# Linear attention's masked level blocks: one strided sum replaced by half masks, an add and four accumulated matmuls

## The reference, cut to what matters

```
G      = cumsum(log_a)                                # per frame and key channel
scores = sum_d q[n,d] * k[m,d] * exp(-|G[n,d] - G[m,d]|)
o      = scores @ v + (q * exp(G)) @ state
state  = exp(G_last) * state + (k * exp(G_last - G))^T @ v
```

## Time and profile before

| what | value |
|---|---|
| median of 3 runs | 2629.23 us |
| profiled execution: span from first to last instruction | 2625.6 us (the page gives no time of it beside the span) |
| mean granted TensorE clock | 0.972 |
| busy, TensorE matmul / weight load | 2446.7 (93%) / 1964.3 us (75%) |
| busy, VectorE | 808.3 us (31%) |
| busy, ScalarE | 402.1 us (15%) |
| busy, GpSimd | 1317.4 us (50%) |

### The profile page before, as it was taken

One profiled execution on the slowest core, in us unless ns is written; L12 is line 12 of the kernel. 1 busy time (PEld: TensorE's weight loads), 2 busy tenths in 40 slices (PEclk: granted clock), 3 DMA queues, 4 the chain that ended last, 5 costly groups with the idle time before them and its releaser, 6 DMA issues. The chain is left out here.

```text
span 2625.6 us, 28086 instructions
## 1 busy us (share of the span) xinstructions
PE 2446.7 (93%) x10712; PEld 1964.3 (75%) x10712; DVE 808.3 (31%) x917; ACT 402.1 (15%) x581; POOL 1317.4 (50%) x711
## 2 busy tenths in 40 slices
PE   6999999999999998766898998898899999999988
PEld 5888788888888887666774664676788888888776
DVE  3000240000000004999327336226532222232333
ACT  3000110010001002222002002002321111111201
POOL 3434343333333333555559598577253333347774
PEclk9999999999999999888999999999999999999999
DMA  4323222222222250121444434444222222234333
GB/s 155 100 92 105 79 95 98 96 96 96 96 96 96 96 209 32 57 71 42 144 161 144 146 126 144 160 140 156 96 83 73 74 74 72 74 133 140 141 121 144
DMA packets 137741, 285.77 MB, mean 109 GB/s; under 512 B 10689, under 2 KB 60097, under 8 KB 137682
## 3 DMA queue, kind: packets, MB, share of 16 engines
q1 hardware_dynamic: 137106, 282.90, 31.0%
q10 hardware_dynamic: 576, 2.10, 0.2%
HBM read 207.36 MB, written 77.59 MB: 109 GB/s over the span
## 5 line engine op out<-in xcount | busy, mean ns | idle before, releaser
L353 POOL TENSOR_TENSOR w_hi<-w_raw,zero_col 128x1024 fp32r<-128x1024 f32 x233 | 448.7, 1926 | 1080.3 <-PE psum L319 1064.6
L317 PE MATMUL psum<-act_hi,w_hi 128*128 128x512 f32 x2128 | 834.0, 392 | 15.5 <-DVE act_lo L386 6.1
L318 PE MATMUL psum<-act_lo,w_hi 128*128 128x512 f32 x2128 | 832.6, 391 | 0.0
L319 PE MATMUL psum<-act_hi,w_lo 128*128 128x512 f32 x2128 | 832.2, 391 | 0.0
L356 POOL TENSOR_TENSOR w_lo<-w_raw,w_hi 128x1024 fp32r<-128x1024 f32 x233 | 576.0, 2472 | 18.3
L317 PEld LDWEIGHTS psum<-act_hi,w_hi 128*128 128x128 f32 x2128 | 402.6, 189 | 102.0 <-issue 14.5
L319 PEld LDWEIGHTS psum<-act_hi,w_lo 128*128 128x128 f32 x2128 | 402.3, 189 | 84.2
L318 PEld LDWEIGHTS psum<-act_lo,w_hi 128*128 128x128 f32 x2128 | 402.6, 189 | 83.7
L863 DVE TENSOR_TENSOR q_lev<-e_t,g_x 128x896 f32<-128x896 f32 x32 | 52.4, 1639 | 660.6 <-ACT e_t L741 660.5
L317 PE MATMUL psum<-w_hi,d_hib 128*128 128x512 f32 x480 | 193.3, 403 | 23.5 <-DVE d_lob L1526 20.6
L318 PE MATMUL psum<-w_lo,d_hib 128*128 128x512 f32 x480 | 192.1, 400 | 0.0
(11 more groups left out here) (137 smaller groups left out, 2162.9 us busy)
## 6 DMA issues: line engine op xcount, KB each, us to landing
w_raw<-in_w_stream SPq DMA_DIRECT2D x233, 512.0 KB, 3.3
proj_scratch<-stage SPq DMA_DIRECT2D x64, 512.0 KB, 2.6
r_x<-proj_scratch SPq DMA_DIRECT2D x64, 256.0 KB, 3.0
value_scratch<-stage SPq DMA_DIRECT2D x24, 512.0 KB, 4.6
ffn_scratch<-u_fb SPq DMA_DIRECT2D x22, 512.0 KB, 2.7
d_raw<-ffn_scratch SPq DMA_DIRECT2D x44, 256.0 KB, 3.6
r_v<-value_scratch SPq DMA_DIRECT2D x32, 256.0 KB, 3.3
x_tok<-in_x SPq DMA_DIRECT2D x4, 1024.0 KB, 8.0
```

The lines of the kernel that those rows point to most:

```text
L317: nc.tensor.matmul(o, s_hi, m_hi, start=start, stop=False)
L318: nc.tensor.matmul(o, s_hi, m_lo, start=False, stop=False)
L319: return nc.tensor.matmul(o, s_lo, m_hi, start=False, stop=stop)
L353: nc.gpsimd.tensor_tensor(w_hi[:, j, :], w_raw[:, j, :], zero_col[:, :].to_broadcast((P, D)), ALU.add).then_inc(sem["hi_split"], 1)
```

## The change

The mask is cut into two instructions of 512 columns. The first writes four masked blocks into `s_sum[:, h, :]`, the second the other four into `s_half`; an add on VectorE puts the second onto the first. The strided sum over the blocks is gone: `outputs` multiplies each of the four remaining blocks with the same values and lets PSUM accumulate them. `s_sum` (512 columns for each of four heads) and `s_half` (512) take the place of `s_masked` (1024) and `p_t` (128 for each head). The waits move: that for the outputs of the tile before stands ahead of the first mask, that for the head before ahead of the second, and TensorE's next scores wait for the second mask. The `begin_phase` of the first head comes ahead of its mask.

```diff
-g_S g_mask g_P g_kT g_kd ...
+g_S g_mask0 g_mask1 g_P g_kT g_kd ...
...
-            s_masked = sb(s, "s_masked", (P, (NL + 1) * P))
+            s_sum = sb(s, "s_sum", (P, HEADS, HALF))
+            s_half = sb(s, "s_half", (P, HALF))
             g_kdt = sb(s, "g_kdt", (P, GLA_QK))
-            p_t = sb(s, "p_t", (P, HEADS, P))
...
                 def scores(h):
                     e = 4 * t + h
                     dve.wait_ge(sem["g_S"], e + 1)
-                    if not (first and h == 0):
-                        dve.wait_ge(sem["g_P"], e)
-                    nc.vector.tensor_tensor(s_masked[:, :], bank[:, 3 * HALF:5 * HALF], masks[:, :],
-                                            ALU.mult).then_inc(sem["g_mask"], 1)
-                    dve.wait_ge(sem["g_mask"], e + 1)
                     if first and h == 0:
                         begin_phase(dve, 2)
                     if not first:
                         dve.wait_ge(sem["g_o"], 2 * t - 1 + h // 2)
-                    nc.vector.tensor_reduce(p_t[:, h, :],
-                                            s_masked[:, :].rearrange("p (l n) -> p n l", n=P),
-                                            AX.X, ALU.add).then_inc(sem["g_P"], 1)
+                    nc.vector.tensor_tensor(s_sum[:, h, :], bank[:, 3 * HALF:4 * HALF], masks[:, 0:HALF],
+                                            ALU.mult).then_inc(sem["g_mask0"], 1)
+                    if not (first and h == 0):
+                        dve.wait_ge(sem["g_P"], e)
+                    nc.vector.tensor_tensor(s_half[:, :], bank[:, 4 * HALF:5 * HALF], masks[:, HALF:2 * HALF],
+                                            ALU.mult).then_inc(sem["g_mask1"], 1)
+                    dve.wait_ge(sem["g_mask0"], e + 1)
+                    dve.wait_ge(sem["g_mask1"], e + 1)
+                    nc.vector.tensor_tensor(s_sum[:, h, :], s_sum[:, h, :], s_half[:, :], ALU.add
+                                            ).then_inc(sem["g_P"], 1)
...
                 for h in (2 * i, 2 * i + 1):
                     o = psum[:, o_bank[i], head_cols(h)]
-                    nc.tensor.matmul(o, p_t[:, h, :], g_v[:, d, h * GLA_DV:(h + 1) * GLA_DV],
-                                     start=True, stop=False)
+                    for l in range(4):
+                        nc.tensor.matmul(o, s_sum[:, h, l * P:(l + 1) * P],
+                                         g_v[:, d, h * GLA_DV:(h + 1) * GLA_DV], start=l == 0, stop=False)
                     last = nc.tensor.matmul(o, q_g[:, d, h, :], g_st[:, h, :], start=False, stop=True)
...
                     if not (first and h == 0):
-                        pe.wait_ge(sem["g_mask"], e)
+                        pe.wait_ge(sem["g_mask1"], e)
                     for l in range(NL + 1):
```

More of the change, by code:

```diff
@@ L154 @@
 g_in0 g_in1 g_gate_in g_tab_in g_tab g_la_hi g_la_lo g_E g_exp g_qG g_dec g_klev g_kend
-g_S g_mask g_P g_kT g_kd g_o g_u g_state g_bn g_mv g_lnv g_rstd g_on g_onT g_og g_hi g_lo
+g_S g_mask0 g_mask1 g_P g_kT g_kd g_o g_u g_state g_bn g_mv g_lnv g_rstd g_on g_onT g_og g_hi g_lo
 r_tab_in r_in0 r_in1 r_in2 r_in3 r_gate_in0 r_gate_in1 r_gate_in2 r_gate_in3 r_xc r_xs r_rope r_qd r_kT r_kd r_S r_P r_o r_u r_state
```

## The result

| | median us | lowest to highest | runs |
|---|---|---|---|
| before | 2629.45 | 2625.99 to 2633.64 | 6 |
| changed | 2637.3 | 2634.35 to 2641.02 | 6 |

The ratio is 1.0028, 95% interval [1.0016, 1.0039]: the changed kernel is slower. The medians are 7.9 us apart (0.30%). That is beyond the 0.2% that the prediction took as what a measurement can tell, though the lower end of the interval, 0.16%, is not. The prediction was 2636.6. A later set of runs of the changed kernel gave 1.0033 [1.0021, 1.0044].

The account below looks back on a forecast made before the run. VectorE's busy time was taken to be partly turns with GpSimd, plus a late exp 1. Tile 0 at 0, tiles 1 to 6 +3.6, tile 7 -0.5 and tail +4.3 gave +7.4 us: 2636.6, own range 2630 to 2643.

Parts of the forecast that it names:

- rival 1: VectorE's queue is the bound and adds are never held, so all savings are kept: -32 us, 2597; chance 0.06.
- the walk: One linear-attention tile followed in time across engines from the gate's end: 30.6 us, +0.2, or up to +1.0 with the load.
- The order of turns: VectorE and GpSimd alternate: head 3's add waits for `act_lo`, then `k_lev` 0 precedes `q_lev` 0; head 1's add waits for `la_lo`.
- Rival 2: Half kept: heads 0 and 2 save 1.25 us each, heads 1 and 3 neither gain nor lose; -8 us, 2621; chance 0.14.
- Masks and add: VectorE per head: two half masks 1.28 us and one add 0.57 us, 1.85 in all, replacing 3.1.
- Tail: Bare outputs and state input after the last tile: matmuls end 5.2 us later, minus 0.9 of slack, +4.3 us.
- Last tile: Tile 7 has no `la_lo` and its head 1 is held less: -0.5 us (-0.9 to -0.1).
- Tile 0 and 1: Tile 0, without outputs, statistics or gate: 0 (-1 to +1); tile 1: +0.6 us like each of tiles 1 to 6.
- The next five tiles: Those after tile 1, at +0.6 us each (bounds +0.2 to +1.0), part of +3.6 for tiles 1 to 6.
- rival 3: TensorE's outputs run at its lower clock level, each group 3.7 us longer, exp 1 as well: 2663 us; chance 0.08.
- The waits and `begin_phase`: Moved waits at the masks: 0 (0 to 0.1 us per head); `begin_phase` ahead of the first mask: 0, at most 1.2 once.
- the late load: Log-decay DMA issued behind the later state input 1: `la_lo` and head 1's add move by up to 0.9 us per tile.

Follow-up runs that it names:

- e7: The changed kernel again, unaltered, on the chip of the mixed kernels, against the kernel before: 2639.62 us, ratio 1.0033.
- e12: Changed kernel with one of four summed blocks multiplied (not the reference's output) and `act_lo` moved behind head 1 of the next tile: 2617.88 us, 0.9949.
- e8: The changed kernel with the log decays loaded a tile earlier, under their own semaphore: 2634.7 us, ratio 1.0014 to the kernel before.
- e4: The changed kernel with TensorE's outputs 0 cut in two around decay 1: 2641.27 us, ratio 1.0043 to the kernel before.
- e9: The changed kernel with outputs 0 cut around decay 1 and log decays loaded a tile earlier: 2633.06 us, ratio 1.0007 to the kernel before.
- e10: Heads 0 and 2 as changed, 1 and 3 as before, with outputs 0 cut around decay 1 and log decays loaded earlier: 2615.83 us, 0.9946.
- e5: Heads 0 and 2 as in the changed kernel, heads 1 and 3 as before: 2625.25 us, ratio 0.9985 to the kernel before.
- e6: Heads 0 and 2 as changed, 1 and 3 as before, with outputs 0 cut around decay 1: 2617.92 us, ratio 0.9957 to the kernel before.
- e3: The changed kernel without the add, all matmuls kept (not the reference's output): 2635.06 us, ratio 1.0026 to the kernel before.

## Why the prediction was right

**The step that decided** was to read the busy time of VectorE in order of time. A sum of durations gives -32 us (rival 1); the walk gave +7.4, and the stage came out at +8.1. The mechanism is borne out; that the figure is met within a microsecond is in part luck, for the stage of e7 came out at +13.2. Its stations against the tile above (T = 0 is 1137.95, 1.19 behind the gate's start as in the walk):

| station | walk | measured |
|---|---|---|
| mask 3 starts | 0.35 | 0.3 |
| head 3's add ends | 3.95 | 4.0 |
| `q_g` 0 ends | 7.4 | 7.3 |
| exp 1 starts | 7.5 | 7.5 |
| `q_g` 1 ends | 12.15 | 11.8 |
| `q_lev` 2 starts | 18.6 | 18.3 |
| head 1's add ends | 24.0 | 24.0 |
| `q_g` 3 ends | 27.5 | 27.4 |
| gate ends | 30.6 | 30.5 |

The order of turns, inferred from few rows, held at head 3 and head 1, and for head 3 e12 shows its cause. Rival 2's sign did not come: of the seven adds of head 3 that have an `act_lo` near them, six took 2.04 to 2.27 us, and the seventh is that of the long tile. At head 1's keys the order was wrong: VectorE's `q_lev` 1 went ahead of `k_lev` 1, and `q_g` 1 ended 0.35 us sooner than walked. Masks and add were sized a little too small, at 1.85 us per head against the measured 1.99.

**The terms.** Tail: +4.3 predicted, +4.4 measured. Last tile: -0.5 predicted, -0.9 measured. Tile 0 and 1: 0 and +0.6 predicted, +0.6 measured. The next five tiles: +3.0 predicted, +4.0 measured, but otherwise made up: four cost +0.3 each in the mean, and one +2.9, through scores 3 at the lower level. The last is of rival 3's kind at a place which the rival did not name: the outputs of that tile ran at a granted clock of 1.00 (1108.9 to 1113.1), and scores 3 at 0.50. That +0.6 for each tile and the mixture of +0.3 and +2.9 come to nearly the same sum is luck. So the term for the tiles was near by its sum, and right by its mechanism only for the part that is even from tile to tile. How often such a tile falls differs between executions (one in the profile here, two in e7's, with 32.3 us each). e7's 13.2 us are 3.1 ahead of the first gate, 3.2 in the five tiles, 2.1 in the last tile and 4.8 in the tail.

**The waits and `begin_phase`** cost nothing that shows: mask 0 of the first tile followed its copy at once.

**What the walk had too small** was the late load. It was given 0.4 per tile; e8 with the load early has tiles 0.6 to 0.7 below the regular ones, and none that is long. Whether the earlier load is also what keeps the long tiles away in e8 is not separated.

**Where a later walk failed** is e4: it moved one of three chains (the held adds, the exponential of head 1, the late load) that end close together and took the whole distance as gain. Only with the load moved as well (e9) did tiles come near 29.3 (29.2 and 29.4), and in the others scores 3 ran at the lower level.

The rule of the Trainium skill (SBUF — State Buffer, "SBUF: two separate sides") on the pair of ports that VectorE with two SBUF inputs shares with GpSimd is borne out by the measurements: the add with two SBUF inputs took 2.26 us beside `act_lo` and 0.69 without (e12), and the strided sum, with one input, ran 1.95 us beside `k_lev` (e10).

## What to carry to other kernels

Ask of each new instruction not only how long it runs but which other engine's instruction it must take turns with: a shorter one with two SBUF inputs can cost more than a longer one with one, and keeping it to where GpSimd is idle turned a loss of 0.3% into a gain of 0.15% (e5), and 0.4% with outputs 0 cut in two as well (e6). Work moved to an engine that looks a third idle still delays what is queued behind it there; walk the queue to the next hand-over before calling it hidden. When a walk shows several chains ending close together, moving one gives the distance to the next, not its own length.

## What was not expected of the hardware

TensorE's level changed the length of single tiles by 2 to 3 us at nearly the same mean clock. In the kernel before, every window of 30 us shows a granted clock of 0.89 and tiles of 30.2 to 30.5 us; in the changed kernel, with 5 us more matmul per tile, the windows show 0.88 to 0.94.

What counts is which group of matmuls the lower level falls on. In the kernel before it is always scores 2, for which VectorE does not wait. Every long tile of the changed kernel, of e3, e4 and e7 (31.7 to 33.2 us), and every tile of 30.8 to 31.0 us in e9, begins with scores 3 wholly or in part at the lower level, 2.3 to 3.06 us of loads against 1.64, after 2.1 to 4.4 us of idle time. The last tiles of e3 and e9 begin so too, at 29.1 and 29.7 us; they have no `la_lo`. That idle time does not decide alone: scores 2 of the long tile ran at full level after 3.31 us of it. What sets the group stays open; no run here changed that alone.
